# A hybrid encoder on one core: the memory laid out by features, its 1/rms through memory as a row and applied by GpSimd, in place of sixteen transposes on TensorE

## The chip, the cores and the metric

The kernel runs on one core of a Trainium2 chip. The metric is the device time of one execution in microseconds (us). A profiled execution has a time of its own and a span, which is the time from its first to its last recorded instruction.

The engines are TensorE (PE in the profile; PEld is its loading of stationary operands), VectorE (DVE), ScalarE (ACT), GpSimd (POOL) and SyncE (SP, here only the issuer of DMAs). Each runs its own instructions in program order, and they wait for each other on semaphores.

## What is computed

Two layers of an encoder over 256 tokens of width 1024, in float32. The stretch of interest is the first layer's beginning and the normed memory, which the cross-attention reads.

```python
def rms_norm(x, g):
    y = x * rsqrt(mean(x * x, axis=-1, keepdims=True) + EPS)
    return y * g

for l in range(2):
    # mixer: one input projection, then mLSTM heads, neighbourhood attention heads, gated linear attention heads
    h = h + hybrid_mixer(rms_norm(h, mix_norm_g[l]), w_in[l], ...)
    # 4-head cross-attention into 256 memory tokens
    mem_n = rms_norm(mem, mem_norm_g[l])          # k = mem_n @ w_xk, v = mem_n @ w_xv
    h = h + memory_cross_attention(rms_norm(h, xattn_norm_g[l]), mem_n, ...)
    h = h + conv_ffn(rms_norm(h, ffn_norm_g[l]), ...)
return rms_norm(h, final_norm_g)
```

The 1/rms of the memory's tokens is the same for both layers; only the gain differs.

## The kernel before

**Matmuls in three.** Each float32 operand is split into a high half (a cast) and a low half (the rest), and each product takes three matmuls: high x high, high x low, low x high. For the weights, ScalarE makes the high half (line 1180) and VectorE the low half (line 1560). Weights come in units of up to 1 MB into a ring of three raw buffers: SyncE loads unit n when the low half of unit n - 3 is done. The units of the first layer are in this order: `gq`, `mix`, `qk0`, `nqk4`, `qk1`, `qk2`, `va`, `vb`, `nq`, `nk`, `gk`, `nva`, `nvb` and so on.

**Order of work.** Every engine has its order written out by hand. On TensorE the first layer goes: the turned tokens, the fills `gq`, `mix`, `qk0`, `nqk4`, a few gate matmuls (849 to 861), the fills `qk1` and `qk2`, the transposes of the memory (872), the fill `v` (two halves), the transposes of the gates (880, 881; they wait for the stabiliser scans of VectorE), decay rows (889) and scores (917) of the first mLSTM heads, the fill `nq`, then per head an output (900), decay rows, scores and one more fill (`nk`, `gk`, `nv`, ...).

**The memory.** SyncE loads it by tokens into `mtm`, which lies in the tile `xk` (line 604). ScalarE squares and sums each half of the tokens and takes the root (1169, 1170; the squares themselves go to `xv` and are not used). VectorE takes the reciprocal (1543) and scales `mtm` by it, token by token (1645). TensorE turns it in 16 transposes into four PSUM banks `mt_0` to `mt_3` (872), and ScalarE copies these to `memT`, features by tokens (1311). Both layers later read `memT` with their gain (1209 on ScalarE, 1596 on VectorE).

**VectorE in this stretch.** Low half of `qk2`, gate copies (1633 to 1640), the memory's scaling, low half of `va`, second convolution (1622, 1626; it waits for ScalarE's part, 1259), low half of `vb`, the stabiliser scans (1650 to 1659, each waits for the one before), two SiLU products (1664), low half of `nq`, the gates' copy from PSUM (1670), then per head four sums (1710 to 1713), four products (1722 to 1725) and a low half.

**GpSimd** makes masks and constants until 27.3 us. After that it has one sum of 640 columns per layer (690).

## Time and profile before

| | us |
|---|---|
| three runs, median | 855.88 |
| lowest and highest | 855.3 and 856.11 |
| the profiled execution's own time | 855.05 |
| its span | 853.2 |
| TensorE busy | 840.2 |
| VectorE busy | 603.0 |
| ScalarE busy | 497.6 |
| GpSimd busy | 23.4 |
| mean granted clock of TensorE | 0.998 of full speed |

The busy times are those of one execution. The profile marks what an engine waited for in square brackets behind a row: `[0.63 <-ACT qk L1259]` is 0.63 us of idle time, ended by ScalarE's write of `qk` at line 1259. `L` numbers are lines of the kernel, `out<-in` the tiles written and read; `bank` is PSUM, `arena` a large SBUF tile that many names share. `xN` says that N neighbouring rows were merged.

### The profile page before, as it was taken

Reading aid. Unit: us, or ns where it says so; the run is one execution under the profiler, and the core shown is the slowest. Engines: PE = TensorE matmul, PEld = TensorE weight load, DVE = VectorE, ACT = ScalarE, POOL = GpSimd, SP = SyncE. Lnnn points to the kernel's source line nnn. Section 1 sums busy time; section 2 is a strip of 40 time slices with the busy share of each in tenths; the row PEclk is TensorE's granted clock in tenths of the full one; section 3 lists DMA queues with packets and bytes.
Section 4 is the critical chain, followed back from the end, with each engine's and each line's share of the span. In section 5 each row is a group of like instructions: output and inputs, shape, how many; then the busy total and the mean of one; then the engine's idle time right before and its main releaser. Section 6 shows DMA issues by size and latency. Waiting matters only on the chain.

```text
span 853.2 us, 14935 instructions
## 1 busy us (share of the span) xinstructions
PE 840.2 (98%) x6302; PEld 780.6 (91%) x6302; DVE 603.0 (71%) x844; ACT 497.6 (58%) x697; POOL 23.4 (3%) x42
## 2 busy tenths in 40 slices
PE   8999999999999999999999999999999899999997
PEld 7999998889899999999999999888998899999996
DVE  5897978769757556656577988887776765656555
ACT  6964763678566444445568646845755654444444
POOL 5200001000000000000000000010000000000000
PEclk9999999999999999999999999999999999999999
DMA  9725653545346565565447356437526455565551
GB/s 324 219 82 175 217 180 117 191 139 198 107 142 227 180 209 177 196 201 195 149 140 239 85 170 210 147 102 247 174 71 197 149 197 190 182 208 176 185 171 50
DMA packets 108618, 147.44 MB, mean 173 GB/s; under 512 B 3272, under 2 KB 88456, under 8 KB 108552
## 3 DMA queue, kind: packets, MB, share of 16 engines
q1 hardware_dynamic: 108408, 146.23, 51.6%
q8 instruction: 50, 0.82, 0.4%
q10 hardware_dynamic: 144, 0.26, 0.1%
q14 instruction: 16, 0.13, 0.1%
HBM read 144.12 MB, written 1.05 MB: 170 GB/s over the span
## 4 chain that ended last, share of the span: by engine, by line
PE 97%; DVE 1%; POOL 1%; ACT 1%; DMA 1%; issue 0%; SPq 0%; DVEq 0%; ACTq 0%; POOLq 0%
PE bank L721 28%; PE bank L722 27%; PE bank L723 27%; PE bank L765 5%; PE bank L808 3%; PE bank L900 2%; PE bank L827 1%; PE bank L917 1%; DMA h<-in_x 1%; PE bank L1090 0%; PE bank L952 0%; PE bank L889 0%; PE bank L935 0%; PE bank L1006 0%; PE bank L1032 0%
## 5 line engine op out<-in xcount | busy, mean ns | idle before, releaser
L1560 DVE TENSOR_TENSOR wlo<-raw,whi 128x2048 fp32r<-128x2048 f32 (+3 forms) x142 | 303.1, 2139 | 106.7 <-ACT whi L1180 105.9
L1180 ACT ACTIVATE whi<-raw 128x2048 fp32r<-128x2048 f32 (+3 forms) x144 | 257.6, 1792 | 59.0 <-PE bank L723 49.7
L721 PE MATMUL bank<-yhi,whi 128*128 128x256 f32 x704 | 195.2, 277 | 0.5 <-DVE ylo L1576 0.5
L722 PE MATMUL bank<-ylo,whi 128*128 128x256 f32 x704 | 194.8, 277 | 0.0
L723 PE MATMUL bank<-yhi,wlo 128*128 128x256 f32 x704 | 194.8, 277 | 0.0
L721 PEld LDWEIGHTS bank<-yhi,whi 128*128 128x128 f32 x704 | 132.3, 188 | 1.7 <-issue 0.7
L722 PEld LDWEIGHTS bank<-ylo,whi 128*128 128x128 f32 x704 | 132.2, 188 | 0.8
L723 PEld LDWEIGHTS bank<-yhi,wlo 128*128 128x128 f32 x704 | 132.4, 188 | 0.0
L721 PE MATMUL bank<-xhi,whi 128*128 128x256 f32 x320 | 91.5, 286 | 1.1 <-DVE xlo L1576 0.9
L721 PE MATMUL bank<-whi,xhi 128*128 128x512 f32 (+2 forms) x256 | 90.1, 352 | 0.0
L723 PE MATMUL bank<-xhi,wlo 128*128 128x256 f32 x320 | 89.1, 279 | 0.0
L722 PE MATMUL bank<-xlo,whi 128*128 128x256 f32 x320 | 89.1, 278 | 0.0
L723 PE MATMUL bank<-whi,xlo 128*128 128x512 f32 (+2 forms) x256 | 88.5, 346 | 0.0
L722 PE MATMUL bank<-wlo,xhi 128*128 128x512 f32 (+2 forms) x256 | 88.4, 345 | 0.0
L722 PE MATMUL bank<-wlo,fhi 128*128 128x512 f32 x176 | 69.0, 392 | 0.0
L721 PE MATMUL bank<-whi,fhi 128*128 128x512 f32 x176 | 68.9, 391 | 0.0
L723 PE MATMUL bank<-whi,flo 128*128 128x512 f32 x176 | 68.6, 390 | 0.0
L721 PEld LDWEIGHTS bank<-xhi,whi 128*128 128x128 f32 x320 | 60.2, 188 | 4.7 <-issue 2.9
L1495 ACT ACTIVATE arena<-bank,pcols 128x256 f32<-128x256 f32 x44 | 22.5, 561 | 68.0 <-PE bank L723 68.0
L723 PEld LDWEIGHTS bank<-xhi,wlo 128*128 128x128 f32 x320 | 60.3, 189 | 0.0
L722 PEld LDWEIGHTS bank<-xlo,whi 128*128 128x128 f32 x320 | 60.3, 188 | 0.0
L721 PEld LDWEIGHTS bank<-whi,xhi 128*128 128x128 f32 x256 | 48.1, 188 | 4.8 <-issue 1.0
(291 smaller groups left out, 1376.0 us busy)
## 6 DMA issues: line engine op xcount, KB each, us to landing
raw<-in_w_up SPq DMA_DIRECT2D x44, 1024.0 KB, 5.0
raw<-in_w_down SPq DMA_DIRECT2D x22, 1024.0 KB, 4.8
raw<-in_w_in SPq DMA_DIRECT2D x10, 1024.0 KB, 5.7
raw<-in_w_xk SPq DMA_DIRECT2D x8, 1024.0 KB, 5.4
raw<-in_w_xv SPq DMA_DIRECT2D x8, 1024.0 KB, 5.4
raw<-in_w_out SPq DMA_DIRECT2D x8, 1024.0 KB, 5.0
raw<-in_w_xq SPq DMA_DIRECT2D x8, 1024.0 KB, 5.8
raw<-in_w_xo SPq DMA_DIRECT2D x8, 1024.0 KB, 5.1
```

The source lines that it names most:

```text
L721: mm(o, s_hi, m_hi, start=first, stop=False, skip_group_check=True)
L722: mm(o, s_hi, m_lo, start=False, stop=False, skip_group_check=True)
L723: return mm(o, s_lo, m_hi, start=False, stop=last, skip_group_check=True)
L765: last = mm(bank(name, 2, T)[:, f, :], w[:, k, f * P:f * P + P], x[:, k, :], start=k + i + f == 0, stop=k == KT - 1 and i == 2, skip_group ...
L808: last = mm(bank(names[t])[:, 0:n], x[:, k, t * P:(t + 1) * P], w[:, k, :], start=k + i == 0, stop=False, skip_group_check=True)
L827: last = nc.tensor.transpose(turned_bank(l, group, k)[:, t * P:(t + 1) * P], tmb[:, t, k * P:(k + 1) * P], ident[:])
L900: last = mm(o[:, t, d, :], w[:, c:c + P], mv[:, jt, g, :], start=i == 0, stop=i == len(src) - 1)
L917: last = mm(bank(f"mls{hh + x}", TT, T)[:, jt, :], qk[r, 3 + j, jt * P:(jt + 1) * P], qk[r, j, :], start=True, stop=True)
L1180: A(weight(whi, gu), raw[:, gu % RING, 0:SIZE[gu]], ACT.Copy).then_inc(hi_done, 1)
L1495: last = A(fy[:, p % 2, f, :], bank(f"fa{p}", 2, T)[:, f, :], ACT.Identity, scale=pcol[:, RA + RB_W + 22 + j:RA + RB_W + 23 + j], bias=pco ...
L1560: tt(weight(wlo, gu), raw[:, gu % RING, 0:SIZE[gu]], weight(whi, gu), ALU.subtract).then_inc(lo_done, 1)
```

## The change

The host hands in a second copy of the memory, transposed: features by tokens. SyncE loads it straight into `memT`. VectorE still takes the reciprocals of the two columns of roots, but no longer scales the memory by tokens. SyncE writes the two columns of 128 values to a scratch tensor in device memory, waits until they have landed, and reads them back as one row of 256 values, repeated on all 128 partitions, into the start of `xv`. GpSimd multiplies `memT` by this row, in place, in one instruction of 128x2048. ScalarE waits for it before the first use of `memT`. The transposes of TensorE, their PSUM banks and the four copies of ScalarE are gone. The memory by tokens is still loaded, for the squares.

SyncE's new issues and waits stand between the load of unit `nq` and that of unit `nk`.

```diff
--- before.py
+++ after.py
@@ -142,9 +142,6 @@
         job(name, b)
     job("qk1", 4, "qk1")
     job("qk2", 5, "qk2")
-    if l == 0:
-        for i in range(4):
-            job(f"mt_{i}", i)
     tm("v", (7, 6))
     job("gt", 4)
     for h in range(MLH + 1):
@@ -217,7 +214,6 @@
 for _l in range(1, DEPTH):
     NA_FILL[_l] = ((), (4,), (5,), (6,), (), (7,), ())
 NA_OUT = (3, 5, 6)
-MT_ORDER = (2, 0, 1, 3)
 NA_PAIRS = ((0, 1), (2, 3), (4,))
 NA_K = range(3, 6)
 XATTN = (("xq", 0), ("xq", 1), ("xq", 2), ("xs", 0), ("xs", 1), ("xq_begun", 3), ("xs", 2), ("xq", 3), ("xt", 0), ("xt", 1),
@@ -230,8 +226,6 @@
     s += ["xk1"] if l else []
     s += ["gq", "mix", "nqk4", "z00", "z01", "z10", "z11"]
     v += ["qk0", "gp", "qk1", "gt"]
-    if l == 0:
-        s += [f"mt_{i}" for i in MT_ORDER]
     s += ["v0", "v1"]
     for h in range(MLH):
         v += [f"mlb{h}"] + (["qk2"] if h == 0 else []) + [f"mls{h}"]
@@ -440,6 +434,7 @@
         zc = tmb[:, 1, :].rearrange("p (a b) -> p a b", b=T)
         xp = tmb[:].rearrange("p t (x n) -> p (t x) n", n=T).rearrange("p (h t) n -> p h t n", t=TT)
         mtm = xk[:].rearrange("p a b -> p (a b)").rearrange("p (t c) -> p t c", t=TT)
+        memrow = xv[:, 0, 0:T]
         gfin = memT[:].rearrange("p a b -> p (a b)")[:, 0:DM]
         mlh = qk[:, 0:3, :].rearrange("p a b -> p (a b)").rearrange("p (t h d) -> p t h d", t=TT, d=DH)
         sq = qk[:, 3:6, :].rearrange("p a b -> p (a b)").rearrange("p (t h d) -> p t h d", t=TT, d=DH)
@@ -478,6 +473,10 @@
         nav_in = sem("nav_in")
         rstd_ready = sem("rstd_ready")
         xn_ready = sem("xn_ready")
+        memroot_ready = sem("memroot_ready")
+        memroot_out = sem("memroot_out")
+        memrow_in = sem("memrow_in")
+        memT_in = sem("memT_in")
         memn_ready = sem("memn_ready")
         mixed_ready = sem("mixed_ready")
         xhi_ready = sem("xhi_ready")
@@ -612,6 +611,14 @@
                         for r in range(GR):
                             o = GW * (r % 2) + KEYS_AT[b]
                             sp.dma_start(nav4[KW * r:KW * r + KW, b, :], nav[o:o + KW, r // 2, :]).then_inc(nav_in, 16)
+                if name == "nk" and l == 0:
+                    sp.dma_start(memT[:], a["mem_by_features"].rearrange("(k p) t -> p k t", p=P)).then_inc(memT_in, 16)
+                    sp.wait_ge(memroot_ready, TT)
+                    v = a["mem_roots"]
+                    for t in range(TT):
+                        sp.dma_start(bass.AP(v.tensor, v.offset + t * P, [[1, P], [1, 1]]), rt[:, t:t + 1]).then_inc(memroot_out, 16)
+                    sp.wait_ge(memroot_out, 16 * TT)
+                    sp.dma_start(memrow, bass.AP(v.tensor, v.offset, [[0, P], [1, T]])).then_inc(memrow_in, 16)
                 if name == "gva" and l + 1 < DEPTH:
                     is_filled(sp, l, "z11")
                     is_drained(sp, l, "mix")
@@ -683,6 +690,10 @@
             sel(win[above, 1, 0:16], ALU.is_ge, NEG, -29, [[4, 16]], -1)
             sel(win[above, 1, :], ALU.is_ge, NEG, 92, [[-4, KW]], 1)
             pool.sem_inc(const_ready, 1)
+
+            pool.wait_ge(memT_in, 16)
+            pool.wait_ge(memrow_in, 16)
+            g.tensor_tensor(memT[:], memT[:], memrow.rearrange("p (o t) -> p o t", o=1).broadcast_to([P, KT, T]), ALU.mult).then_inc(memn_ready, 1)
 
             for l in range(DEPTH):
                 pool.wait_ge(drained["D"], DRAIN[l, "ga0"][1])
@@ -862,16 +873,6 @@
                         last.then_inc(te_done, 1)
                 fm_blocks("qk1", "n1", [(0, 4 if l else 0, KT), (1, 0, KT)])
                 fm_unit("qk2", "n1")
-                if l == 0:
-                    pe.wait_ge(memn_ready, TT)
-                    for i in range(4):
-                        free(f"mt_{i}")
-                        for kk in range(2):
-                            for t in range(TT):
-                                k = 2 * i + kk
-                                last = nc.tensor.transpose(bank(f"mt_{i}", 2, T)[:, kk, t * P:(t + 1) * P],
-                                                           mtm[:, t, k * P:(k + 1) * P], ident[:])
-                        last.then_inc(te_done, 1)
                 tm_unit("v", ("v0", "v1"), ML, "n1")
 
                 free("gt")
@@ -1305,10 +1306,6 @@
                 silu_tanh(0)
                 silu_tanh(1)
                 split_hi("nq")
-                if l == 0:
-                    for i in MT_ORDER:
-                        is_filled(act, l, f"mt_{i}")
-                        drain(A(memT[:, 2 * i:2 * i + 2, :], bank(f"mt_{i}", 2, T), ACT.Copy))
                 for t in range(TT):
                     is_filled(act, l, f"v{t}")
                     drain(A(mv[:, t, :, 0:DH], bank(f"v{t}")[:, 0:ML].rearrange("p (h d) -> p h d", d=DH), ACT.Copy))
@@ -1359,6 +1356,8 @@
                             last.then_inc(np_ready, 1)
                     if hh == 0:
                         is_used(act, l, "gga")
+                        if l == 0:
+                            act.wait_ge(memn_ready, 1)
                         memory_hi("mem", l, range(4))
                         take("gg0")
                         is_used(act, l, "ggb")
@@ -1641,8 +1640,8 @@
                 if l == 0:
                     dve.wait_ge(mem_in, 16 * TT)
                     for t in range(TT):
-                        inverse_root(t)
-                        ts(mtm[:, t, :], mtm[:, t, :], rt[:, t:t + 1], None, ALU.mult).then_inc(memn_ready, 1)
+                        root_ready(t)
+                        V.reciprocal(rt[:, t:t + 1], rt[:, t:t + 1]).then_inc(memroot_ready, 1)
                 split_lo("va")
                 conv(1)
                 split_lo("vb")
@@ -2050,6 +2049,7 @@
     laid_out = {name: inputs[name] for name in _INS}
     laid_out["params"] = parameter_columns(inputs, np)
     laid_out["na_bias"] = neighbour_bias(inputs["na_rpb"], np)
+    laid_out["mem_by_features"] = inputs["mem"][0].T
     laid_out["w_few"] = few_columns(inputs["w_in"], np)
     for name, v in laid_out.items():
         v = np.ascontiguousarray(v)
@@ -2057,6 +2057,7 @@
             v = v[0]
         arrays[f"in_{name}"] = v
         aps[name] = nc.dram_tensor(f"in_{name}", v.shape, mybir.dt.from_np(v.dtype), kind="ExternalInput").ap()
+    aps["mem_roots"] = nc.dram_tensor("mem_roots", (TT, P), F32, kind="Internal").ap()
     out = nc.dram_tensor("out", (T, DM), F32, kind="ExternalOutput").ap()
     build(nc, aps, out)
     r = run_bass_kernel_spmd(nc, [arrays], core_ids=[0])
```

## Rows read from the trace of the kernel before

**Rows 1.** the page: busy us of each engine (share of the span), instructions.

```profile
PE 840.2 (98%) x6302; PEld 780.6 (91%) x6302; DVE 603.0 (71%) x844; ACT 497.6 (58%) x697; POOL 23.4 (3%) x42
```

**Rows 2.** waits of TensorE: us in total, times, the longest.

```profile
PE bank L827 <- DVE tmb L1547: 2.9, 2, 1.7
```

**Rows 3.** timeline of TensorE: start us, duration us, instruction; xN were merged.

```profile
37.70 1.91 PE L872 MATMUL bank<-ident,xk 128*128 128x128 f32 x16
39.36 0.42 PE L721 MATMUL bank<-whi,xhi 128*128 128x384 f32 x1
47.87 0.27 PE L880 MATMUL bank<-ident,arena 64*128 64x64 f32 x1
48.68 1.13 PE L917 MATMUL bank<-qk 64*128 64x256 f32 x8
49.75 0.39 PE L721 MATMUL bank<-xhi,whi 128*128 128x256 f32 x1
```

**Rows 4.** timeline of VectorE, 32 to 54 us; in brackets its idle time before.

```profile
33.15 0.76 DVE L1645 TENSOR_SCALAR xk<-xk,rt 128x1024 f32<-128x1024 f32 x1
34.68 1.75 DVE L1560 TENSOR_TENSOR wlo<-raw,whi 128x1536 fp32r<-128x1536 f32 x1
37.06 0.87 DVE L1622 SCALAR_TENSOR_TENSOR qk<-bank,pcols,qk 128x255 f32<-128x255 f32 x2 [0.63 <-ACT qk L1259]
45.23 0.42 DVE L1659 TENSOR_TENSOR gsplit<-arena,gsplit 64x256 fp32r<-64x256 f32 x1
45.68 1.29 DVE L1664 SCALAR_TENSOR_TENSOR qk<-arena,qk 128x512 f32<-128x512 f32 x2
46.89 2.29 DVE L1560 TENSOR_TENSOR wlo<-raw,whi 128x2048 fp32r<-128x2048 f32 x1
49.09 0.42 DVE L1670 COPY gt<-bank 128x256 f32<-128x256 f32 x1
53.61 2.28 DVE L1560 TENSOR_TENSOR wlo<-raw,whi 128x2048 fp32r<-128x2048 f32 x1
```

**Rows 5.** timeline of ScalarE: the memory's copies, and the first use of memT.

```profile
46.36 2.03 ACT L1311 ACTIVATE memT<-bank 128x512 f32<-128x512 f32 x4
103.02 1.30 ACT L1209 ACTIVATE xhi<-memT,pcols 128x256 fp32r<-128x256 f32 x3
```

**Rows 6.** SyncE's issue, and DMA issues of a stretch: KB each, us to landing.

```profile
30.71 0.37 SPq L584 DMA_DIRECT2D raw<-in_w_in  x1
raw<-in_w_in SPq DMA_DIRECT2D x1, 1024.0 KB, 6.4
out<-tmb SPq DMA_DIRECT2D x3, 256.0 KB, 2.0
```

**Rows 7.** timelines of GpSimd and VectorE; one tile's instructions (ns min/median/max).

```profile
11.86 2.40 POOL L657 TENSOR_TENSOR wlo<-raw,whi 128x1024 fp32r<-128x1024 f32 x1
L642 POOL TENSOR_SCALAR_AFFINE_SELECT win<-win x8: 194/210/2257, 22.5 to 27.0; 64x32 f32<-64x32 f32 x6, 64x16 f32<-64x16 f32 x2
23.84 2.29 DVE L1560 TENSOR_TENSOR wlo<-raw,whi 128x2048 fp32r<-128x2048 f32 x1 [3.19 <-ACT whi L1180]
19.35 1.30 DVE L1560 TENSOR_TENSOR wlo<-raw,whi 128x1024 fp32r<-128x1024 f32 x1 [2.48 <-ACT whi L1180]
136.79 3.55 POOL L690 TENSOR_TENSOR arena<-arena 128x640 f32<-128x640 f32 x1 [109.54 <-DVE arena L1822]
136.63 2.28 DVE L1560 TENSOR_TENSOR wlo<-raw,whi 128x2048 fp32r<-128x2048 f32 x1
```

**Rows 8.** timelines of VectorE and TensorE around the nva split.

```profile
67.76 2.88 DVE L1560 TENSOR_TENSOR wlo<-raw,whi 128x1280 fp32r<-128x1280 f32 x2
69.62 0.39 PE L721 MATMUL bank<-whi,xhi 128*128 128x320 f32 x1
```

**Rows 9.** windows at the end: engines' busy us (instructions), granted clock, DMA share, GB/s.

```profile
847.00:847.50 0.50, 0.28 (x2) 0.00 (x0) 0.46 (x2) 0.47 (x3) 0.00 (x0) 1.00 0.00 0
849.00:849.50 0.50, 0.00 (x0) 0.00 (x0) 0.29 (x2) 0.27 (x2) 0.00 (x0) 0.80 0.44 172
```

## The prediction, made before the changed kernel ran

> **What bounds the kernel now.** I read the page first. TensorE is busy for 98% of the span [rows 1]. The list of who waits for whom, cut to TensorE, then has little in it: its longest entry is the wait for the normed tokens at the two layer starts [rows 2]. So a microsecond taken out of TensorE's stream is a microsecond of time, if what the next matmuls need is ready that much earlier. The page can't say whether it is. The timelines of the stretch where the transposes stand do, engine by engine.
>
> TensorE runs the 16 transposes from 37.70, starts the `v` fill at 39.36, the gate transposes at 47.87, the scores at 48.68 and the `nq` fill at 49.75, with no idle time between [rows 3]. VectorE is as full: after a short wait for ScalarE at 37.06 it works without a gap to the end of the low half of `nq` at 46.89 + 2.29 = 49.18 [rows 4]. That is only 49.75 - 49.18 = 0.57 us before TensorE uses it. In this stretch two engines are nearly critical, and VectorE is the one that the change doesn't relieve.
>
> **The change, part by part.**
>
> TensorE loses the 16 transposes: 39.36 - 37.70 = 1.66 us of its path [rows 3]. Their work hid nothing that `v` needs: the low half of `va` ends at 34.68 + 1.75 = 36.43, before 37.70 [rows 4]. `v` then starts at 37.70 and ends at 46.2.
>
> VectorE loses two scalings, 1.5 us together, and keeps the two reciprocals [rows 4]. This gives nothing behind it: they stand before 37.06, where VectorE waits for the convolution on ScalarE, and ScalarE's work ahead of that is unchanged. So from 37.06 its times are those of before.
>
> ScalarE loses four copies, 2.03 us at 46.36 [rows 5]. They stand behind the high half of `nq` and ahead of work that waits for VectorE, so this brings no more than slack.
>
> The naive gain is thus cut at once. With VectorE unchanged the `nq` fill can start some 0.05 to 0.1 us after 49.18, and not at 49.75 - 1.66 = 48.09. What is late next is the low half of `nq`, and of 1.66 us about 0.5 stays.
>
> SyncE gets four DMAs and two waits between the loads of `nq` and `nk`. The `nq` load is issued at 30.71 and lands 6.4 us later, at 37.1 [rows 6]. The memory by features, 1 MB, is issued right behind it, about 31.1. A MB at the rate of these loads takes some 3 us, so it lands at about 39 to 41. The two root columns are issued when VectorE has made the reciprocals, at about 33.3, but their data stand behind that MB on the same queue. The trace has no store of 4-byte pieces. The nearest row is the store of 256 KB, which lands in 2.0 us [rows 6]. From 33.3 alone that would be 35.3, behind the MB it is 41 to 42; I take 41.5. Then comes the row, 128 KB, at 2 to 3.5 us: 44. The bounds are 41 and 47. Queued behind the two waits on SyncE is the load of `nk`, issued at about 36.5 before (the low half of `va` frees its slot) and at about 42 now; it lands at 47 to 48. ScalarE wants it at 47.2 with the copies gone, 49 with them, so this costs nothing up to a landing at 49. The new wait of ScalarE for `memT` costs nothing either: it first reads it at 103.02 [rows 5].
>
> GpSimd gets one product of 128x2048 from two SBUF operands, in place. Its product of 128x1024 took 2.40 us, so 2048 columns take 4.8. The product of 128x640 at 136.79 ended at 140.34; if it ran only once VectorE's split had ended at 138.9, it took 1.4 us, which makes 4.6 for 2048 [rows 7]. I take 4.7, from about 44 to 49. GpSimd has nothing else to do then.
>
> The question is what this product does to VectorE. The rows show that the two engines exclude each other. A select of 64x32 takes 0.2 us on GpSimd, but one that met VectorE's split at 23.84 (two SBUF operands, until 26.13) took 2257 ns: it was held until the split was over [rows 7]. The other way round there is one faint trace: the split of 128x1024 at 19.35 took 1.30 us, and 2.29/2 + 0.08 = 1.22 would be usual. Selects were running on GpSimd then [rows 7]. No row shows a long GpSimd instruction in front of VectorE, so the cost has to be bounded: nothing, if VectorE always goes first, up to the whole 4.7 us, if GpSimd once in holds the path for its whole instruction. I take the whole. VectorE was held off by a short one for about what was left of it, and GpSimd was held off by VectorE for a whole instruction.
>
> The rule of the Trainium skill, page "SBUF — State Buffer", section "Who interferes with whom", says the same and more sharply: a VectorE instruction with two SBUF inputs and a GpSimd instruction that reads SBUF exclude each other, whoever issues first keeps the shared port for the whole instruction, and the other fully blocks. By that rule the time is the one that I forecast; without it this change would be worth half a microsecond. The page "GPSIMD Engine Reference", section "3.1 Elementwise — side-by-side cycle accounting", has 4497 ns for an elementwise sum of 2048 columns; by that the sum would be 0.2 us smaller.
>
> VectorE's work between 40 and 49 is of just that kind: stabiliser scans, sums and products on SBUF tiles, then the low half of `nq`. In the scans each instruction waits for the one before, and there is a gap between them (45.23 + 0.42 = 45.65, and the next starts at 45.68), in which the waiting product gets in. Only the SiLU products and the split follow each other without a gap (46.89 is before 45.68 + 1.29 = 46.97) [rows 4]. If the product gets in at about 44, everything behind it on VectorE moves by 4.7 us. The scans end at 45.65 + 4.7 = 50.35, and TensorE, done with `v` at 46.2, waits 4.1 us for them with the gate transposes. The SiLU ends at 51.7, the low half of `nq` at 53.9, and the fill starts at 53.95.
>
> The sum on TensorE's path: 53.95 - 49.75 = +4.2 us, the 1.66 already in it. Then VectorE is 4.7 us later and TensorE 4.2, so the slacks behind shrink by 0.5. The narrowest is that of `nva`, whose low half ends at 67.76 + 1.44 = 69.20 for a fill at 69.62 [rows 8]: 0.2 us more. And TensorE idles for 4.1 us. After the last matmul of the trace, at 847.28, the granted clock was still whole until about 849.3, and then half, 1.2 GHz [rows 9]. So it will fall in this wait. The gate transposes, decay rows and scores (1.9 us) then take up to 3.8, mostly hidden behind the split; the `nq` fill (5.5 us) could double at worst. No row shows the clock coming back; between 0 and 5.7 us I take 0.8, near the low end, since the engine works from 50.4 on. Together 4.2 + 0.2 + 0.8 = +5.2 us.
>
> The profiled execution took 855.05 us for its span of 853.2; plus 5.2 it is 860.3. It lies 0.83 us below the median of the three runs, 855.88, so for the median I predict 861.1.
>
> **The rivals.**
>
> *GpSimd comes too late or is kept out* (the other side, no slower). If the row lands after VectorE has begun the `nq` split at 46.9, or if waiting GpSimd never wins a gap of 0.03 us, the product starts at 49.2. There VectorE reads PSUM and at most one SBUF tile until 53.61 [rows 4], and splits with such operands ran beside GpSimd unharmed. The product ends at 53.9 and takes 0.3 us from the `nk` split, which has slack. The gain is the 0.5 us, at 855.4. For it: my landing time is built from two DMAs of a kind that the trace lacks, in series, and 3 us more decide it. Against it: VectorE has gaps from 40 to 45.7, and the landing most likely falls there.
>
> *The port isn't held for the whole product.* If it is shared piece by piece, VectorE loses 1 to 3 us of the 4.7, TensorE 0.5 to 2.5 after the 0.57: 856.4 to 858.4.
>
> *The slack isn't what the rows say and the transposes are pure gain.* 1.66 us less: 854.2. Against it stands the end of the `nq` split at 49.18, which nothing in the change moves earlier.
>
> *The round trip through memory holds the weights up.* From a landing of the roots past 44, `nk` lands past 49.5 and ScalarE's exponential of the first head slips, then VectorE's products; each microsecond past it costs nearly one. Should the 4-byte store take 5 us more, this gives about 859 without any port conflict.
>
> **How the numbers follow.** GpSimd in front of VectorE 0.54, shared or shorter holds 0.07, the round trip 0.02, kept out or late 0.33, the full gain 0.04. A measurement of this kernel tells about 0.2% (1.7 us) from no change, so the first lies above that, and most of the second and third. Slower 0.61, same 0.37, faster 0.02 (the full gain is 0.19%, at the edge). The forecast's own range is 859.4 (no clock loss, 855.3 + 4.1) to 864. As "kept out" has a third of the chance, the range must reach it: 854.8 to 863.5.
>
> **What would show it.** In the trace after: one VectorE instruction between 40 and 47 that takes about 4.7 us more than its size asks, beside GpSimd's product; TensorE waiting for the gate transposes for about 4 us, then again for the `nq` split; the granted clock at half in between. Kept out, the product instead takes 5 to 9 us and ends near 54, and TensorE waits 1.1 us before `nq`. I am wrong if the row lands after 47, or if VectorE's rows keep their lengths beside the product.

## The result, and the profile after

The changed kernel took 858.99 us (median of five runs, 858.29 to 861.55) beside 855.84 for the kernel before (854.82 to 856.11 on the same chip). By the medians that is 3.15 us slower. The ratio over all the runs is 1.005, with a 95% interval of 1.0040 to 1.0061, which is 4.3 us (3.4 to 5.2): two of the five runs, at 860.54 and 861.55, lie well above the median. Forecast were 861.1, or +5.2. The profiled execution took 858.99, with a span of 857.4 against 853.2.

The page of the changed kernel, busy us of each engine:

```profile
PE 841.5 (98%) x6286; PEld 781.4 (91%) x6286; DVE 601.8 (70%) x842; ACT 496.4 (58%) x693; POOL 28.1 (3%) x43
```

Beside [rows 1], VectorE has lost its two scalings, ScalarE its copies, and GpSimd has gained 4.7 us. TensorE has 16 instructions fewer and yet 1.3 us more busy time.

GpSimd's product is the first thing to look for. Timelines of the changed kernel, GpSimd, then VectorE (start us, duration us; in brackets the idle time before); the last row is the first head product in the kernel before:

```profile
49.83 4.62 POOL L696 TENSOR_TENSOR memT<-memT,xv 128x2048 f32<-128x2048 f32 x1 [22.56 <-DMA xv<-mem_roots]
46.90 2.28 DVE L1559 TENSOR_TENSOR wlo<-raw,whi 128x2048 fp32r<-128x2048 f32 x1
51.77 0.87 DVE L1625 SCALAR_TENSOR_TENSOR qk<-bank,pcols,qk 128x255 f32<-128x255 f32 x2
56.18 0.42 DVE L1721 SCALAR_TENSOR_TENSOR arena<-bank,arena 128x256 f32<-128x256 f32 x1 [3.54 <-ACT arena L1322]
52.55 0.41 DVE L1722 SCALAR_TENSOR_TENSOR arena<-bank,arena 128x256 f32<-128x256 f32 x1
```

The product started at 49.83, when the scans and the low half of `nq` were done, and lay beside work with a PSUM operand. From 37.06 to 49.2 VectorE's rows are those of [rows 4] within 0.02 us, and no row beside the product is longer than usual. Nothing was held: the expected conflict did not happen. VectorE lost its time later: its first head product starts at 56.18, 3.54 us idle before it, where before it started at 52.55.

The bracket sends us to ScalarE, and its bracket to a load. Timeline of ScalarE, then of SyncE's issue, the landings (KB each, us from issue to landing), and SyncE's wait (us in total, times, longest), all of the changed kernel; the last row is ScalarE's high half of `nk` in the kernel before:

```profile
53.29 1.93 ACT L1181 ACTIVATE whi<-raw 128x2048 fp32r<-128x2048 f32 x1 [5.91 <-DMA raw<-in_w_in]
31.14 0.58 SPq L615 DMA_DIRECT2D memT<-in_mem_by_features  x1
33.22 1.15 SPq L619 DMA_DIRECT2D mem_roots<-rt  x2
44.35 0.32 SPq L621 DMA_DIRECT2D xv<-mem_roots  x1
44.72 5.08 SPq L583 DMA_DIRECT2D raw<-in_w_in  x3
mem_roots<-rt SPq DMA_DIRECT2D x2, 0.5 KB, 9.4
xv<-mem_roots SPq DMA_DIRECT2D x1, 128.0 KB, 5.3
raw<-in_w_in SPq DMA_DIRECT2D x1, 1024.0 KB, 8.6
SPq L621 <- DMA mem_roots<-rt: 10.0, 1, 10.0
49.01 1.95 ACT L1180 ACTIVATE whi<-raw 128x2048 fp32r<-128x2048 f32 x1
```

SyncE stood for 10.0 us at the wait for the two stores of 512 bytes. They landed 8.1 and 10.7 us after their issue (the 9.4 of the row is the middle of the two). Only then, at 44.72, could it issue the load of `nk`, some 8 us later than the kernel before, which issued it at about 36.5 and had it 5.0 us later. Now it took 8.6 us and landed at 53.3; ScalarE had been ready since 47.4.

What TensorE then did, first its waits, then the clock in windows (engines' busy us, granted clock, DMA share, GB/s), then the first matmuls behind:

```profile
PE bank L901 <- DVE arena L1724: 2.4, 1, 2.4
PE bank L732 <- DVE wlo L1559: 1.0, 2, 0.6
42.00:43.00 1.00, 1.00 (x8) 1.00 (x7) 0.93 (x3) 0.98 (x2) 0.00 (x0) 1.00 0.00 0
60.00:61.00 1.00, 1.00 (x6) 1.00 (x6) 1.00 (x2) 0.00 (x0) 0.00 (x0) 0.50 0.46 35
63.00:64.00 1.00, 1.00 (x11) 1.00 (x11) 0.38 (x2) 1.00 (x3) 0.00 (x0) 1.00 0.09 15
59.68 0.55 PE L732 MATMUL bank<-xhi,whi 128*128 128x256 f32 x1 [0.45 <-DVE wlo L1559]
60.46 0.41 PE L732 MATMUL bank<-xhi,whi 128*128 128x256 f32 x1
```

TensorE waited 2.4 us for the first head's products, worked, waited 0.45 for the low half of `nk`, and ran the first three us of that fill (up to about 62.6) at half clock, 1.2 GHz: a matmul each 0.21 us in place of 0.114. From 63 the clock was whole again. The fall itself lies at 59.2 (mean granted clock 0.59 from 59 to 60): 1.8 us after the wait of 2.35 us had ended, and not behind the wait of 0.45, which only began then. The window from 42 stands for the stretch from 39 to 45: the load of `memT` was over, and while SyncE still waited for its stores the DMA engines moved next to nothing (share 0.00, 0 GB/s).

Set side by side by TensorE's small matmuls, which both timelines show, the loss builds up so (changed kernel minus before): gate transposes -1.08 us, first head's output +1.88, second head's output +4.05, and +4.05 to the end of the layer. The steps: 0.59 of wait for `nq` and 2.35 for the first output make the 2.96 between the first two marks; the wait of 0.45, about 1.5 of half clock and 0.2 that I did not place make the 2.17 between the next two. The loss is complete at 67 us; nothing that follows adds to it.

### The profile page after: what moved, and what is told of

The parts are those of the page before. It is cut to its first block, busy times and chain, and to the rows that moved or that the text cites. A ratio compares the mean times of both kernels' runs of the same rounds, so it can differ in the third digit from the quotient of the medians.

```text
span 857.4 us, 14903 instructions
## 1 busy us (share of the span) xinstructions
PE 841.5 (98%) x6286; PEld 781.4 (91%) x6286; DVE 601.8 (70%) x842; ACT 496.4 (58%) x693; POOL 28.1 (3%) x43
## 4 chain that ended last, share of the span: by engine, by line
PE 91%; DMA 3%; DVE 2%; ACT 2%; issue 1%; POOL 1%; SPq 0%; POOLq 0%; ACTq 0%
PE bank L732 26%; PE bank L733 25%; PE bank L734 25%; PE bank L776 5%; PE bank L819 3%; PE bank L901 2%; DMA mem_roots<-rt 1%; DMA raw<-in_w_in 1%; PE bank L838 1%; PE bank L918 1%; ACT whi L1181 1%; DMA h<-in_x 1%; DVE wlo L1559 1%; PE bank L1091 0%; PE bank L953 0%
```

## The experiments

All times are medians, with the interval of the ratio to the kernel before on the same chip. An offset is a mark of TensorE's timeline against the kernel before. It belongs to the one profiled execution, which can lie a microsecond or more from the median: 1.2 us below it in e6, 1.6 below in e5, 2.5 above in e7.

### Where the round trip stands, and the product without it

**e2_early_product**: no round trip; GpSimd multiplies by a tile of ones as soon as `memT` has landed (the 1/rms is left out).

```diff
-                    sp.wait_ge(memroot_ready, TT)
-                    ... (the stores and the row)
-            pool.wait_ge(memrow_in, 16)
-            g.tensor_tensor(memT[:], memT[:], memrow ...
+            g.tensor_tensor(memT[:], memT[:], ones[:].rearrange("p (o t) -> p o t", o=1).broadcast_to([P, KT, T]), ALU.mult)
```

> The changed kernel without the trip: GpSimd multiplies memT by a row of ones as soon as memT has landed, at about 39, in the middle of VectorE's scans. It leaves out the 1/rms of the memory. The forecast's mechanism (GpSimd's product, once in, holds VectorE off for its whole length): an instruction of VectorE between 40 and 46 takes 4 to 4.6 us more, the nq split ends near 53.8, TensorE idles for 3.5 us at the gate transposes, and the time is 4 to 6 us above the kernel before, 860 to 862. The rival (VectorE goes first, or both share): VectorE's rows keep their lengths, the product stretches to 6 to 14 us, and the time is 0.3 to 1 us below the kernel before.

Measured 860.44 (1.0045 to 1.0075), +4.9 us. GpSimd, VectorE and TensorE in its timeline, and a window with the granted clock:

```profile
39.87 5.13 POOL L689 TENSOR_TENSOR memT<-memT,ones 128x2048 f32<-128x2048 f32 x1 [12.60 <-DMA memT<-in_mem_by_features]
38.75 1.75 DVE L1552 TENSOR_TENSOR wlo<-raw,whi 128x1536 fp32r<-128x1536 f32 x1
40.42 4.85 DVE L1642 SCALAR_TENSOR_TENSOR arena<-arena 64x256 f32<-64x256 f32 x1
50.23 0.34 PE L874 MATMUL bank<-ident,arena 64*128 64x64 f32 x1 [3.46 <-DVE gsplit L1651]
53.75 0.55 PE L725 MATMUL bank<-xhi,whi 128*128 128x256 f32 x1
50.00:51.00 1.00, 0.77 (x5) 0.69 (x6) 0.97 (x3) 0.00 (x0) 0.00 (x0) 0.50 0.00 0
```

An instruction of 0.41 us ([rows 4] has its neighbour at 0.42) took 4.85: it was held until GpSimd's product was over. TensorE waited 3.5 us at the gate transposes, the clock fell to half, the `nq` fill began at 53.75 (forecast: 53.95), and the offset was +4.80 from the first head's output on (forecast: +5.2). This is the forecast's mechanism with its size; the product only has to come early. And it got in between two instructions that follow each other without a gap (38.75 + 1.75 = 40.50 is past 40.42), where the prediction had counted on a gap.

The Trainium skill, page "SBUF — State Buffer", section "Who interferes with whom", says that a VectorE instruction with two SBUF inputs and a GpSimd instruction that reads SBUF exclude each other, and that the one which issues first keeps the shared port for its whole instruction. The row of 4.85 us agrees.

**e3_no_product**: the same without the product (the memory isn't normed).

> The changed kernel without the trip and without the product; it leaves out the 1/rms of the memory. Only the transposes, the copies and the scalings are gone and the memory by features is loaded. Every theory: TensorE comes 1.1 to 1.66 us earlier to the gate transposes and then waits for the nq split, which ends at 49.2 as before; 0.3 to 0.6 us below the kernel before, 855.2 to 855.6. If the slack behind isn't what the rows say: 854.2.

Measured 855.29 (0.9988 to 1.0006), -0.2 us. Its waits of TensorE:

```profile
PE bank L723 <- DVE wlo L1550: 1.2, 1, 1.2
```

The gate transposes stand at -1.92, the `nq` fill waits 1.16 us for its low half, and from there the offset is -0.83, from `nva` on -0.50. So in the trace taking out the transposes is worth half a microsecond, as the prediction worked out, and not 1.66; the medians can't tell it from nothing.

**e4_trip_alone**: the kernel before, with the round trip at the place where the change has it, and its row used by nobody.

```diff
+                if name == "nk" and l == 0:
+                    sp.wait_ge(memn_ready, TT)
+                    ... (two stores, the wait for them, the row)
```

> The kernel before, with the trip alone added at the place where the change has it: two stores of 128 values, the wait, the row read back into an unused tile, then the load of nk. The transposes stay, no memory by features, no product. If the stores of 4-byte pieces are slow by themselves: they land 8 to 10 us after their issue also without 1 MB in front of them, nk is issued at 43 to 45, and the time is 2 to 3 us above the kernel before, 857.8 to 859. If they were slow only because they stood behind the 1 MB: they land in 2 to 4 us, nk is issued by 39 and the time is that of before.

Measured 856.82 (1.0008 to 1.0027), +1.3 us. SyncE's stores, the landings of the round trip (the row's is the least, 5.5; the stores' are the others), and ScalarE:

```profile
34.92 0.82 SPq L622 DMA_DIRECT2D mem_roots<-rt  x2
DMA to landing us min/median/max: 5.5/6.3/8.2
51.81 1.92 ACT L1190 ACTIVATE whi<-raw 128x2048 fp32r<-128x2048 f32 x1 [2.55 <-DMA raw<-in_w_in]
```

Without the 1 MB in front the stores still took 6.3 and 8.2 us. `nk` was issued at 43.84, as expected, and landed at 51.8, and the offset grew to +1.86. The time missed both ranges that I had written down (2 to 3 us above, or none): the loss was smaller. But the MB ahead in the queue is at most a part; the stores are slow without it.

**e6_trip_no_product**: the changed kernel, only GpSimd's product left out (the memory isn't normed).

> The changed kernel without GpSimd's product, the trip and all else as they are; it leaves out the 1/rms of the memory. Theory 1 (the whole loss is the trip's): the time is that of the changed kernel, 3 to 3.5 us above the kernel before, 858.5 to 859.3. Rival (the product has a part in it): 1 us or more below the changed kernel.

Measured 858.23 (1.0019 to 1.0041), +2.8 us. TensorE's longest wait for the first head:

```profile
PE bank L898 <- DVE arena L1722: 1.3, 1, 1.3
```

The row was issued at 43.21, `nk` landed at 51.96 and the offset ended at +2.02; the clock stayed whole. The time falls between the two ranges that I had written down. e3 is the same kernel without the trip, at -0.2: so the trip alone costs about 3 us, which is the greater part of the change's loss. What is left for the product is 0.35 us by the medians and 1.7 by the ratios (1.0050 and 1.0030, whose intervals just touch). Where a trace can be read it costs nothing: no VectorE row is longer beside it in the changed kernel, and e8 below, which has it and issued the row at the same 43.2, ends at +2.17. For the slower executions of the changed kernel, which have no trace, this stays open.

### The product again, at other places

**e1_late_trip**: the whole round trip moved from ahead of the load of `nk` to ahead of that of `nva`.

```diff
-                if name == "nk" and l == 0:   (behind the load of memT: wait, stores, wait, row)
+                if name == "nva" and l == 0:
+                    ... (the same lines)
```

> The changed kernel with the roots' trip through memory (two stores, the wait, the row) moved behind the load of gk, ahead of the load of nva. The memory by features is still loaded at its place. Theory 1 (the trip holds the load of nk up on SyncE): nk is issued at about 36, lands before 43, the waits of TensorE for the first head's output (2.35 us) and for the nk split (0.45) go, the granted clock stays whole, and the time is 0.3 to 1 us below the kernel before, 855.0 to 855.6. Theory 2 (GpSimd's product is what costs): the product still runs, only later, at 53 to 62, among VectorE's SBUF work, and the time stays 2 us or more above the kernel before.

Measured 860.12 (1.0037 to 1.0070), +4.6 us. `nk` was now issued at 35.05 and nobody waited for it, as the first theory asks. But the row landed at 54.9, and then the second came true:

```profile
54.96 5.32 POOL L697 TENSOR_TENSOR memT<-memT,xv 128x2048 f32<-128x2048 f32 x1 [27.77 <-DMA xv<-mem_roots]
53.53 2.28 DVE L1560 TENSOR_TENSOR wlo<-raw,whi 128x2048 fp32r<-128x2048 f32 x1
55.73 5.10 DVE L1664 SCALAR_TENSOR_TENSOR qk<-arena,qk 128x512 f32<-128x512 f32 x1
PE bank L902 <- DVE arena L1725: 3.3, 1, 3.3
```

A SiLU product of 0.69 us took 5.10 behind GpSimd's, again between two instructions without a gap. TensorE waited 3.3 us and worked at half clock from 66 to 72 (granted 0.50 in the windows there); the offset behind it is +5.95. The stall of the trip was exchanged for that of the product.

**e5_nk_first**: the load of `nk` ahead of the stores, `gk` behind them, the row ahead of `nva`.

> The changed kernel with nk loaded first: the two stores stand ahead of the load of gk, and the wait for them with the row ahead of the load of nva. Nothing on SyncE is queued behind the trip that is due. Theory 1 (in the changed kernel only the late load of nk costs, the product is free there): the row lands at 48 to 50, the product runs from 49.2 beside VectorE's reads of PSUM and is over at 54, nk is there in time, and the time is 0.2 to 0.6 us below the kernel before, about 855.1 where that has 855.5. Rival (the product costs wherever it stands among VectorE's work, as behind the late trip): an instruction of VectorE is held for 4 to 5 us, 859 to 860.

Measured 859.02 (1.0025 to 1.0052), +3.6 us; a clear miss of what I expected of it. The product started at 50.88, 1 us later than in the changed kernel, and its end ran into the next low half:

```profile
50.88 4.63 POOL L699 TENSOR_TENSOR memT<-memT,xv 128x2048 f32<-128x2048 f32 x1 [23.69 <-DMA xv<-mem_roots]
53.53 4.13 DVE L1562 TENSOR_TENSOR wlo<-raw,whi 128x2048 fp32r<-128x2048 f32 x1
```

The split took 4.13 us in place of 2.28: it ended 2.15 us past the product's end at 55.51, as if it had started there. TensorE waited 1.3 us for it, and the granted clock was 0.50 to 0.57 from 58 to 61. The offset went from -0.72 at the first head's output to +2.54 at the second. The changed kernel's product, from 49.83 to 54.45, would have run into that split as well, by 0.9 us, had `nk` been there in time; it was harmless because VectorE stood idle from 52.6 to 56.2, for want of `nk`.

### The clock

**e7_keep_clock**: the changed kernel with 22 extra matmuls, whose result nobody reads, where TensorE waits for the first head's output.

```diff
+                    if l == 0 and g == 0:
+                        free(f"mlo{g}")
+                        keep_clock(22, bank(f"mlo{g}"))
                     is_drained(pe, l, f"mls{g}")
```

> The changed kernel with 22 matmuls of 128 columns into a free bank ahead of the first head's output, where TensorE otherwise idles for 2.35 us; nothing is left out. If 1.6 us of the loss are the clock's fall in that wait: the granted clock stays whole, the nk fill runs at its usual pitch, and the time is 1 to 1.6 us below the changed kernel, about 857.4. If the clock isn't part of it: no change, 858.5 to 859.3, or above if the added matmuls last longer than the wait.

Measured 859.38 (1.0039 to 1.0067). Around and behind the filler the clock was whole, but the filler was too long for its hole, since each float32 matmul runs as two. And in the profiled execution the clock had already fallen before it, in the `nq` fill:

```profile
56.32 5.07 PE L712 MATMUL bank<-ident 128*128 128x128 f32 x44
50.00:51.00 1.00, 1.00 (x7) 1.00 (x6) 1.00 (x4) 0.00 (x0) 1.00 (x1) 0.50 1.10 375
```

The filler ended at 61.2, where the changed kernel had the first output at 57.39. Some 1.5 us of that are not its own: `nq` had been waited for 1.16 us, the clock fell at 49.3 and came back at 52.8, and so the filler began at 56.32 where the shorter one of e8 began at 54.83. Behind the same wait of 1.16 us ahead of `nq` the clock stayed whole in e1, e3, e6 and e8. The execution took 861.91 us, 2.5 above the median, and its clock fell once more at 670.6; the other three, at 859.04 to 859.49, have mean granted clocks of 0.998 to 1.000 against its 0.995. The run tells little of what half clock costs behind the first head, so the filler was made shorter.

**e8_keep_clock_short**: the same with 10.

> The changed kernel with 10 extra matmuls on TensorE (keep_clock, 128x128 of float32) put in the wait ahead of the first head's output, 2.3 us by the 5.07 us that 22 of them took. The wait there was 2.4 us, so they should just fill it. If half the clock behind the wait is what the changed kernel pays beyond its wait, the granted clock stays whole from 55 to 64, the nk fill runs at full pitch, and the time is 1 to 1.6 us below that of the changed kernel (858.99), at 857.4 to 858.0. If the half clock is hidden behind VectorE's work anyway, or something else makes up the second part of the loss, it stays at 858.5 to 859.3.

Measured 857.76 (1.0011 to 1.0032), 1.2 us below the changed kernel, and the intervals of the two ratios don't meet. Filler and a window behind it:

```profile
54.83 2.39 PE L712 MATMUL bank<-ident 128*128 128x128 f32 x20
60.00:61.00 1.00, 1.00 (x11) 1.00 (x10) 0.96 (x4) 0.00 (x0) 0.00 (x0) 1.00 1.00 340
```

The fill of `nk` ran at full pitch, 11 matmuls in a microsecond in place of 6. The offset ended at +2.17. This is as the clock term asks, but it is no clean proof: in this execution the row was issued at 43.22 and not at 44.35, so TensorE's hole was smaller, and e6 with the same 43.2 kept its clock without any filler (offset +2.02). Together the executions show this. In e6 VectorE's first head product was 2.30 us later than before (54.85) and the loss 2.02. In the changed kernel it was 3.63 later (56.18) and the loss 4.05. By e6's proportion 3.2 of that belong to the late weights alone, by its difference of 0.28 between the two 3.35, and 0.7 to 0.9 are left for the half clock. This is an estimate from two executions. By it the 1.5 us that the slow matmuls took more are partly hidden; that TensorE would else have come early to the next head's products is an argument, not shown.

### What is slow in a store of 512 bytes

**e9_stores**: the kernel before, and behind its last load five DMAs, each alone.

```diff
+            for o, w in ((0, 1), (P, 16), (32 * P, P)):
+                sp.dma_start(bass.AP(v.tensor, v.offset + o, [[w, P], [1, w]]), ident[:, 0:w]).then_inc(probe, 16)
+                ... (wait for it)
+            sp.dma_start(xk[:, 0, :], bass.AP(v.tensor, v.offset + 32 * P, [[0, P], [1, T]])).then_inc(probe, 16)
+            ... (wait for it; then the same from in_x)
```

> The kernel before, with five DMAs of SyncE behind the last load of its stream, each issued only when the one ahead has landed: stores of a tile's first 4, 64 and 512 bytes on each of 128 partitions to a scratch tensor in memory, then a row of 256 values read back repeated on 128 partitions, once from what was just written and once from an input that nobody wrote. It computes all that the kernel before does, and these DMAs besides. If pieces of 4 bytes are slow in themselves, the first store takes 6 to 8 us from issue to landing and the others 2 to 3. If what held the stores in the changed kernel was the queue or the other traffic, all three take 2 to 3 us. If reading what was just written is slow, the first row takes 5 us and the second 3; if the repeated row is slow in itself, both take the same.

Measured 855.3 in one run: these DMAs are off the path. KB and us to landing:

```profile
probe<-ident SPq DMA_DIRECT2D x1, 0.5 KB, 7.4
probe<-ident SPq DMA_DIRECT2D x1, 8.0 KB, 1.4
probe<-ident SPq DMA_DIRECT2D x1, 64.0 KB, 3.0
xk<-probe SPq DMA_DIRECT2D x1, 128.0 KB, 2.8
xk<-in_x SPq DMA_DIRECT2D x1, 128.0 KB, 3.1
```

128 pieces of 4 bytes took 7.4 us with an empty queue; sixteen times the data in pieces of 64 bytes took 1.4. The repeated row takes about 3 us, just written or not, where it took 5.3 in the changed kernel. There the load of `nk` was issued 0.4 us behind it. In e5 the next load came 1.4 us behind the row, and the row took 3.0; in e1 and e4, where it came 0.4 behind, 5.2 and 5.5. That fits loads that hinder each other, but no run was made for it.

**e10_pieces**: four stores in another order, to part the size of a piece from where it goes.

```diff
+            for o, w, step in ((0, 16, 16), (32 * P, 1, P), (16 * P, 1, 1), (20 * P, 1, 16)):
+                sp.dma_start(bass.AP(v.tensor, v.offset + o, [[step, P], [1, w]]), ident[:, 0:w] ...
```

> The kernel before, with four stores of SyncE behind the last load of its stream, each issued when the one ahead has landed, in another order than in e9_stores: 128 pieces of 64 bytes side by side; 128 pieces of 4 bytes, 512 bytes apart in memory; 128 pieces of 4 bytes side by side, as the changed kernel writes its roots; 128 pieces of 4 bytes, 64 bytes apart. It computes all that the kernel before does, and these stores besides. If the 7.4 us of e9_stores belonged to whichever DMA comes first, the first takes 7 us here and the rest 1.4 to 3. If they belong to pieces of 4 bytes as such, the last three take 7 us each. If they come from many pieces written side by side into the same short stretch of memory, only the third takes 7 us.

One run, 855.54 us; the stores are off the path. Landings, in the order of issue (windows of the trace; the last row is the fourth store):

```profile
probe<-ident SPq DMA_DIRECT2D x1, 8.0 KB, 1.4
probe<-ident SPq DMA_DIRECT2D x1, 0.5 KB, 1.4
probe<-ident SPq DMA_DIRECT2D x1, 0.5 KB, 7.4
probe<-ident SPq DMA_DIRECT2D x1, 0.5 KB, 3.6
```

64-byte pieces 1.4 us; 4-byte pieces 512 bytes apart 1.4; 4-byte pieces side by side 7.4; 64 bytes apart 3.6. So neither being first nor the small piece costs the 7 us: it is many small pieces that fall into the same short stretch of memory. For the 4-byte pieces: the closer they lie, the longer it takes.

The Trainium skill, page "DMA: Bandwidth & Descriptors", section "Specifications", says that below 512 bytes the DMA reads, modifies and writes back. Pieces that share a stretch and must take turns at it would give just this order of times; but no run looks inside, and the section has no price for it; the 64-byte pieces, which are below 512 bytes too, show nothing of it at 1.4 us.

### A version that beats both

**v1_squares_late**: everything of the memory later: squares behind the high half of `nq`, round trip with its stores ahead of load `gvb` and its row ahead of `oa`, product after the mLSTM heads.

> A version meant to keep the whole 1.66 us. ScalarE squares the memory behind the high half of nq and no longer ahead of va, so that the second convolution and with it VectorE's scans and the nq split come up to 1.9 us earlier. VectorE takes the reciprocals in the second head, SyncE issues the stores ahead of the load of gvb and the row ahead of that of oa, and GpSimd's product waits for the split of oa, behind which VectorE idles for 4 us. If the slack of 0.57 us in the nq split is what cuts the gain: the nq split ends near 47.3, TensorE doesn't wait for it, and the time is 1.3 to 1.8 us below the kernel before, about 853.9 where that has 855.5. If another wait takes its place: 0.5 us below or less.

Measured 856.63 (1.0007 to 1.0025), +1.2 us, where I had expected 0.5 to 1.8 us less than the kernel before. VectorE was 1.5 us earlier at the `nq` split, but ScalarE paid:

```profile
46.03 1.28 ACT L1175 ACT_TABLE_LOAD   x1
51.58 1.28 ACT L1320 ACT_TABLE_LOAD   x1
53.96 0.42 DVE L1720 SCALAR_TENSOR_TENSOR arena<-bank,arena 128x256 f32<-128x256 f32 x1 [2.81 <-ACT arena L1326]
```

The root between two stretches of other functions costs two table loads; with the squares that is some 5.3 us on ScalarE ahead of the first exponential, and VectorE waited 2.81 us for it. TensorE waited 1.1 us for ScalarE's copies of `v`, which stand behind the squares.

**v2_squares_early**: the squares in ScalarE's idle time near 14 us, the reciprocals between the low halves of `nqk4` and `qk1`, the stores ahead of `nva`, the row ahead of `nvb`, the product held until a split in the attention stage.

```diff
                 split_hi("qk0")
+                if l == 0:   (ScalarE: wait for mem, square_all twice; taken out further down)
                 split_lo("nqk4")
+                if l == 0:   (VectorE: the two reciprocals; taken out ahead of split_lo("va"))
+            pool.wait_ge(lo_done, UNIT[0, "oa"] + 1)
             g.tensor_tensor(memT[:], memT[:], memrow ...
```

> A version meant to beat both. ScalarE squares the memory in its idle time near 15 to 18 us, VectorE takes the reciprocals between the low halves of nqk4 and qk1, so VectorE is some 1.5 to 2 us earlier at the nq split and ScalarE needs no further table loads there. The root stores stand ahead of load nva and the row ahead of load nvb, where a late landing holds up no load that is wanted soon; the product waits for the first split after the mLSTM heads, so that it cannot meet VectorE's scans. If TensorE's slack at the nq split is what eats the 1.66 us of the transposes, this takes 1.3 to 1.8 us less than the kernel before. If VectorE gives its time back at the head products or at nva (0.4 us of slack), no more than 0.5 us is left. If the earlier squares hold up the weight high halves of the start, it is slower by up to 2 us.

Measured 853.2 (852.76 to 853.83), ratio 0.9972 (0.9961 to 0.9984): 2.5 us faster than the kernel before and some 5.7 faster than the changed one. One of its squares, the `nq` split, the stores and the product:

```profile
15.75 1.04 ACT L1174 ACTIVATE xv<-xk 128x1024 f32<-128x1024 f32 x1
44.95 2.28 DVE L1563 TENSOR_TENSOR wlo<-raw,whi 128x2048 fp32r<-128x2048 f32 x1
39.01 1.72 SPq L620 DMA_DIRECT2D mem_roots<-rt  x2
81.44 4.62 POOL L700 TENSOR_TENSOR memT<-memT,xv 128x2048 f32<-128x2048 f32 x1 [54.28 <-DVE wlo L1563]
```

The `nq` split starts 1.94 us earlier than in [rows 4] and TensorE has no wait for it. The product lies in a hole of VectorE's, which is idle for 4.1 us up to 85.4. The offset is -1.64 from the first head's output on and -1.76 at the end: now the 1.66 us of the transposes is real. The medians show 0.7 us more than that, within the interval (1.4 to 3.3 us faster).

## Why the prediction was right and wrong

**Right: what bounds the kernel, and the naive gain.** That only about 0.5 of the 1.66 us survives, because the low half of `nq` ends at 49.18, is e3's wait of 1.2 us and its offset of -0.50; v2, which moves that split, shows the other side of it.

**Right in kind and size, wrong in this kernel: VectorE held by the product.** That VectorE would be held for GpSimd's whole instruction, e2, e1 and e5 show, with +4.8 us in e2 against the forecast +5.2. In the changed kernel it did not occur. So the forecast's direction was met by another mechanism, by luck: the nearness of +5.2 to the measured +3.15 (+3.9 for the profiled executions) proves nothing for its steps, and neither does it that the time lies between 854.8 and 863.5, a range drawn for two other courses of events. It is the rival that I gave 0.02, the round trip holding the weights up, that took place. The "about 859" which stood there is what was measured, but in part by luck too: it was worked out for a store 5 us slower, and the stores were 2.8 us late; the rest came from the load of `nk`.

**Small slips of the working.** The slacks behind were to shrink by 0.5 us against 0.42 at `nva`, which leaves 0.1 and not 0.2; e2 shows nothing there (+4.80 at the first head, +4.81 from the second on). That only the SiLU products and the split follow each other without a gap was a misreading: the low half of `vb` and the instruction behind it, the first of the scans' chain, do so too, and it is there that the product got in (e2). And the range ends at 863.5, though the forecast's own ran to 864.

**The step that failed: the landing of the roots.** I took 41.5 for the roots and 44 for the row, from the 256 KB store's 2.0 us [rows 6] and the MB ahead, with a bound of 47. Measured: 44.3 and 49.7. Three terms of that chain were too small. The two stores took 8.1 and 10.7 us, and the row that I took as the nearest was the wrong yardstick: 256 KB in long pieces says nothing of 512 bytes in pieces of 4 side by side (e9, e10). The row took 5.3, not 2 to 3.5; with the stores this put the product at 49.83, behind the `nq` split and not among the scans. And the `nk` load took 8.6, where I had counted 5 to 6, issued right behind the row, with two more loads behind it (x3 in its row); with the stores this put its landing at 53.3, not at 47 to 48.

**The threshold was right, its chance was not.** "this costs nothing up to a landing at 49" and "from a landing of the roots past 44, ... each microsecond past it costs nearly one" fit: roots at 44.3, `nk` at 53.3. The working had the roots' landing at 41.5 and the point of decision at 44, 2.5 us apart, with a DMA in between whose price no row had. A chance of 0.02 did not fit such a margin; "the row lands after 47" had been written down as what would break the forecast, and was given a third, but all of it was put on the harmless side (the product late, 855.4). I had not joined the two: what makes the row late makes `nk` late as well, since both stand behind the same wait on SyncE.

**The clock.** Forecast was a loss of 0.8 behind a wait of 4.1 us, picked near the low end of 0 to 5.7. e2, which ran the forecast's course, has its `nq` fill at +4.00 and the first head's output at +4.80: 0.8, a lucky pick. In the changed kernel the clock fell after another wait, of 2.35 us, and cost some 0.7 to 0.9 of the 4.05 by the estimate under e8.

**A difference that is not the change's.** In the profiled execution of the changed kernel matmuls of 128x256 stand 0.119 us apart from 30 us on (29.77, 29.89, 30.01 ...), 0.113 in the kernel before (29.76, 29.87, 29.98 ...). TensorE is already 0.28 us behind at 25.7, ahead of anything that the change touches. So the gate transposes stand at -1.08, where e1, e3 and e8 have -1.93, -1.92 and -1.87. In the `nq` fill it is the other way round: 0.118 us apart in the kernel before, 0.1135 in the changed one. The granted clock is whole in all four stretches. It cost nothing, because `nq` was waited for anyway. Its cause stays open.

## What to carry to other kernels

Follow a wait that is put into the stream of a DMA issuer to everything queued behind it: here 10 us at one wait delayed no reader of the data waited for, but the weights behind it. A small vector written to memory in pieces of 4 bytes side by side took 5 to 11 us to land in every run here; keep it off a path with a due time, and place it ahead of loads that are wanted late, as v2 does. Pieces 512 bytes apart landed in 1.4 us (e10), but no version of the kernel was built that way. And a long GpSimd instruction with SBUF operands should be given a start (a wait on something of VectorE's) in a stretch where VectorE reads PSUM or idles. Left to whenever its data lands, it cost nothing at 49.83 in the changed kernel, where VectorE idled behind its PSUM work, and about 3 us at 50.88 in e5, where VectorE's next split was due.

## What I had not expected of the hardware

- Stores of 128 pieces of 4 bytes to device memory, time to landing: side by side 7.4 us with nothing else moving (two in a row 6.3 and 8.2, behind 1 MB 8.1 and 10.7), 64 bytes apart 3.6, 512 bytes apart 1.4; 128 pieces of 64 bytes side by side 1.4.
- GpSimd gets in between two VectorE instructions that overlap at their joint (e1, e2), not only in a gap; one that is already running is left alone.
- The length of TensorE's last wait does not tell whether its clock falls. It fell after 2.35 us (changed kernel, at 59.2), after 1.28 (e5, at 58.1) and in one execution after 1.16 (e7, at 49.3). It stayed whole behind the same wait of 1.16 us in e1, e3, e6 and e8, and in e6 also behind a further one of 1.27 (granted clock 1.00 from 54 to 63).
- The landings of the same two stores differ by a microsecond between executions: the row behind them was issued at 44.35 (changed kernel), 43.57 (e7), 43.22 (e8) and 43.21 (e6). The changed kernel's five runs lie 3.3 us apart, those of the kernel before beside them 1.3.
